# Output projection of the gated convolution: two pairs of tiles direct, six in Strassen's form

## The reference, cut to what matters

```python
def conv_mixer(h, w_in, conv_w, w_out):
    u, b_gate, c_gate, z = jnp.split(h @ w_in, 4, axis=-1)
    y = b_gate * causal_depthwise_conv(c_gate * u, conv_w)
    return (y * jax.nn.silu(z)) @ w_out
...
        x = x + rms_norm(y, norm_post[layer])
        h = rms_norm(x, xattn_norm_pre[layer])
        m = rms_norm(mem, mem_norm[layer])
        y = memory_cross_attention(h, m, m_w_q[layer], m_w_kv[layer], m_w_o[layer])
```

## Time and profile before

| What | us |
| --- | --- |
| Median of three runs | 2331.9 |
| Profiled execution | 2331.37 |
| Its span, first to last instruction | 2329.6 |
| Input projection in Strassen's form | about 1426 to 1977 |
| Output projection, direct | 1977.7 to 2153 |
| Norm, then opening of the cross attention's projection | 2153 to 2159.4 |

### The profile page before, as it was taken

How to read it: one execution, slowest core, us unless ns; L and a number is a source line. 1 busy time by engine, 2 the same in 40 slices (tenths; PEclk the granted TensorE clock), 3 DMA queues, 4 the chain that set the end, 5 groups by cost and what they waited for, 6 DMA issues and landing times.

```text
span 2329.6 us, 31140 instructions
## 1 busy us (share of the span) xinstructions
PE 2292.6 (98%) x12121; PEld 1919.0 (82%) x12121; DVE 1572.5 (68%) x2133; ACT 952.5 (41%) x1573; POOL 276.3 (12%) x213
## 2 busy tenths in 40 slices
PE   8999999999999999999999899999999999999998
PEld 6888888888787778888877788888888888888776
DVE  6676767674455658733385699888988898533855
ACT  5233333323344437522244364444444445322444
POOL 4000000001010101001040330000000100010400
PEclk9999999999999999999999899999999999999999
DMA  5322222223322324442222246767676666423222
GB/s 205 100 78 82 77 81 77 81 79 99 109 91 73 91 67 160 158 168 94 96 71 66 82 154 172 200 191 199 189 199 190 190 189 204 159 91 117 68 68 91
DMA packets 96958, 288.42 MB, mean 124 GB/s; under 512 B 18336, under 2 KB 21568, under 8 KB 96832
## 3 DMA queue, kind: packets, MB, share of 16 engines
q1 hardware_dynamic: 88288, 255.74, 33.0%
q0 software_dynamic: 8064, 29.36, 7.2%
q10 hardware_dynamic: 480, 1.59, 0.2%
HBM read 275.63 MB, written 11.03 MB: 123 GB/s over the span
## 4 chain that ended last, share of the span: by engine, by line
PE 95%; DVE 3%; ACT 1%; issue 1%; DMA 0%; POOL 0%; DVEq 0%; SPq 0%; ACTq 0%
PE acc L1154 17%; PE acc L1156 17%; PE acc L1155 17%; PE m L1649 10%; PE acc L1649 5%; PE m L1654 5%; PE acc L1654 3%; PE acc L1512 2%; PE acc L1513 2%; PE acc L1517 2%; DVE weights_lo L1681 1%; PE m L1328 1%; PE m L1336 1%; PE acc L1382 1%; PE acc L1384 1%
## 5 line engine op out<-in xcount | busy, mean ns | idle before, releaser
L1154 PE MATMUL acc<-input_hi_lo,weights_hi 128*128 128x512 f32 (+1 forms) x1880 | 743.0, 395 | 11.2 <-DVE weights_lo L1681 10.5
L1156 PE MATMUL acc<-input_hi_lo,weights_lo 128*128 128x512 f32 (+1 forms) x1880 | 720.3, 383 | 0.0
L1155 PE MATMUL acc<-input_hi_lo,weights_hi 128*128 128x512 f32 (+1 forms) x1880 | 719.5, 383 | 0.0
L1681 DVE TENSOR_TENSOR weights_lo<-weights_raw,weights_hi 128x1024 fp32r<-128x1024 f32 x288 | 399.4, 1398 | 178.7 <-ACT weights_hi L610 177.9
L1154 PEld LDWEIGHTS acc<-input_hi_lo,weights_hi 128*128 128x128 f32 x1880 | 354.1, 188 | 90.0 <-issue 14.8
L1156 PEld LDWEIGHTS acc<-input_hi_lo,weights_lo 128*128 128x128 f32 x1880 | 353.7, 188 | 71.2
L1155 PEld LDWEIGHTS acc<-input_hi_lo,weights_hi 128*128 128x128 f32 x1880 | 354.5, 189 | 64.6 <-issue 1.9
L610 ACT ACTIVATE weights_hi<-weights_raw 128x1024 fp32r<-128x1024 f32 x288 | 299.1, 1058 | 189.6 <-PE acc L1156 156.6
L1649 PE MATMUL m<-input_hi_lo,weights_hi 128*128 128x512 f32 x672 | 169.3, 394 | 1.2 <-issue 0.9
L1649 PEld LDWEIGHTS m<-input_hi_lo,weights_hi 128*128 128x128 f32 x672 | 120.7, 189 | 24.3 <-issue 2.6
L990 ACT ACTIVATE weights_hi<-weights_raw 128x1024 fp32r<-128x1024 f32 x85 | 89.9, 1059 | 88.6 <-PE m L1654 43.9
(11 more groups left out here) (376 smaller groups left out, 3455.4 us busy)
## 6 DMA issues: line engine op xcount, KB each, us to landing
weights_raw<-in_ab_w_in SPq DMA_DIRECT2D x126, 512.0 KB, 3.5
weights_raw<-in_c_w_in SPq DMA_DIRECT2D x73, 512.0 KB, 4.6
work<-in_c_w_in SPq DMA_DIRECT2D x42, 512.0 KB, 3.7
weights_raw<-in_m_w_kv SPq DMA_DIRECT2D x32, 512.0 KB, 3.6
weights_raw<-in_ab_w_out SPq DMA_DIRECT2D x32, 512.0 KB, 4.4
weights_raw<-in_m_w_q SPq DMA_DIRECT2D x32, 512.0 KB, 3.5
weights_raw<-in_c_w_out SPq DMA_DIRECT2D x32, 512.0 KB, 4.3
weights_raw<-in_c_w_in POOLq DMA_DIRECT2D x29, 512.0 KB, 7.5
```

Of the source, the lines that this page charges most:

```text
L1154: pe.matmul(out, w_hi[:, o:o + P], hi(kt), start=kt == first_kt, stop=False)
L1155: pe.matmul(out, w_hi[:, o:o + P], lo(kt), start=False, stop=False)
L1156: last = pe.matmul(out, w_lo[:, o:o + P], hi(kt), start=False, stop=kt == last_kt)
L1681: TTO(w_lo[:, s * CW:(s + 1) * CW], raw[:, c * CW:(c + 1) * CW], w_hi[:, s * CW:(s + 1) * CW].bitcast(F32), ALU.subtract).then_inc(lo_read ...
```

## The change

- The output projection runs pairs 0 and 1 directly and pairs 2 to 7 in Strassen's form. These are numbered q = 28 to 33, after the 28 of the input projection, and use the same functions, buffers, banks and semaphores. The host lays `c_w_out` out so that the halves of a pair are contiguous.
- While the two direct pairs run, VectorE and ScalarE make the sums of the input y (`turned_sums_out`, `turned_low_out`, `turned_high_out`, and `fourth_low_out` in the first Strassen pair), in X and in parts of Y and the work buffer.
- GpSimd issues the DMA sums of these pairs between its additions of squares: those of pair q after the squares of pair q - 2 have been added. ScalarE makes the squares of a pair during products 2 and 3 of the next one.
- The residual is reloaded in two halves: tiles 0 to 7 after product 2 of the last pair, 8 to 15 after its product 4. VectorE waits for the first half ahead of the first sum with the residual and GpSimd for the second ahead of tile 8.
- The first chunks of the next projection (C_Q1 on) are loaded and split during the last pair; the third is split after its last product. `last_chunk` isn't used here any more.

```diff
-C_Q1, P_Q1 = C_OUT1 + 32, P_OUT1 + 8
+C_Q1, P_Q1 = C_OUT1 + 8, P_OUT1 + 2
...
-S_PAIRS = 28
+S_PAIRS, OUT_PAIRS = 28, 6
...
+            def after_pairs(end, c):
+
+                q = end - 2 + c % 2
+                sp.wait_ge(s_lo, 7 * q + (5 if c < 2 else 3))
+                sp.wait_ge(s_sum["S4" if c < 2 else "S2"], q + 1)
...
-                if n == 0:
-                    sp.wait_ge(s_used, 7 * (S_PAIRS - 1) + 5)
+            for q in range(S_PAIRS, S_PAIRS + OUT_PAIRS):
+                s_loads(q)
+            for c in (0, 2, 1, 3):
+                j, kt0 = opening_chunk(c)
+                after_pairs(S_PAIRS + OUT_PAIRS, c)
+                load(dram["m_w_q"], 16 + 4 * j + kt0 // 4, C_Q1 + c)
+                if c == 2:
                     sp.wait_ge(x_kept, 16 * KT)
-                    for k in range(KT):
+                    sp.wait_ge(s_used, S_ALL - 7 + 3)
+                    for k in range(8):
                         sp.dma_start(xt(k), dram["x_kept"][k]).then_inc(x_back, 16)
-            sp.wait_ge(s_lo, S_CHUNKS)
+            sp.wait_ge(s_used, S_ALL - 7 + 5)
+            for k in range(8, KT):
+                sp.dma_start(xt(k), dram["x_kept"][k]).then_inc(x_back2, 16)
+            sp.wait_ge(s_lo, S_ALL)
...
+            def wino_out():
+
+                OA.round(2)
+                split(C_OUT1 + 4)
+                for n in (2, 0, 1):
+                    turned_high_out(0, n)
+                split(C_OUT1 + 5)
+                split(C_OUT1 + 6)
+                for n in (2, 0, 1):
+                    turned_high_out(1, n)
+                act.wait_ge(turn_in, 16)
+                for k in (0, 1):
+                    out_squares(k, (acc_free, 2 * P_OUT1 + k + 1))
+                split(C_OUT1 + 7)
+                for i in range(S_CHUNKS, S_CHUNKS + S_SLOTS):
+                    s_split(i)
+                for i in range(S_CHUNKS, S_ALL):
+                    q, pos = divmod(i, 7)
+                    n = q - S_PAIRS + 2
+                    product_copy(i, [(turn_lo, 16)] + ([OG("a11", 2)] if n == 7 else []))
+                    if i > S_CHUNKS and i + 2 < S_ALL:
+                        s_split(i + 2)
+                    if n == 2 and pos in (1, 2):
+                        turned_high_out(pos - 1, 3)
+                    if pos in (2, 3):
+                        k = 2 * n - 4 + pos
+                        if n == 7 and pos == 2:
+                            act.wait_ge(s_used, S_ALL - 7 + 2)
+                        out_squares(k, (acc_free, 2 * (P_OUT1 + 2)) if n == 2 else (s_ev, evacs(q - 1, "C21")))
+                    if i >= S_ALL - 2:
+                        act.wait_ge(s_used, i)
+                        split(C_Q1 + i - S_ALL + 2)
+                q = S_PAIRS + OUT_PAIRS - 1
+                out_squares(14, (s_ev, evacs(q, "C12")))
+                out_squares(15, (s_ev, evacs(q, "C21")))
+                act.wait_ge(s_used, S_ALL)
+                split(C_Q1 + 2)
...
-            out_phase(2, C_OUT1, P_OUT1, 4, lambda kt: YV(f"lo{kt}"))
+            NM.round(2)
+            for n in range(2):
+                for c in range(4):
+                    chunk(C_OUT1 + 4 * n + c, P_OUT1 + n, OUT1_TILES[c], KT - 1,
+                          ready=(lambda kt: YV(f"lo{kt}")) if n == 0 else None, first_kt=OUT1_TILES[0])
+            for q in range(S_PAIRS, S_PAIRS + OUT_PAIRS):
+                for pos in range(7):
+                    wino_product(q, pos)
+            pe.wait_ge(*OG("a13", 2))
+            ss_part(acc_sq, True, False).then_inc(*NM.did("last0"))
...
+            def wino_out():
+                turned_sums_out(0)
+                split(C_OUT1 + 5)
+                take_out(0)
+                turned_sums_out(1)
+                split(C_OUT1 + 6)
+                turned_low_out(0)
+                split(C_OUT1 + 7)
+                turned_low_out(1)
+                for i in range(S_CHUNKS, S_CHUNKS + S_SLOTS):
+                    s_split(i)
+                take_out(1)
+                for i in range(S_CHUNKS, S_ALL):
+                    if i > S_CHUNKS:
+                        evacuate_product((i - 1) // 7, (i - 1) % 7)
+                        if i + 2 < S_ALL:
+                            s_split(i + 2)
+                    q, pos = divmod(i, 7)
+                    if pos in (0, 2):
+                        weight_sum(q, ("S2", "S4")[pos // 2])
+                    if q == S_PAIRS and pos in (1, 2):
+                        fourth_low_out(pos - 1)
+                    if i >= S_ALL - 2:
+                        split(C_Q1 + i - S_ALL + 2)
+                evacuate_product(S_PAIRS + OUT_PAIRS - 1, 6)
+                split(C_Q1 + 2)
...
                 for k in range(KT - 2):
+                    if r == 2 and k >= 2 and k % 2 == 0 and k // 2 <= OUT_PAIRS:
+                        wino_sums(S_PAIRS + k // 2 - 1)
                     pool.wait_ge(*OA(f"s{k}", r))
```

More of the change, by code:

```diff
@@ L504, in cross_loads @@
             def cross_loads(l):
-                for c in range(16):
+                for c in range(4 * l, 16):
                     j, kt0 = opening_chunk(c)
@@ L535, in s_loads @@
                 s_load(q, 2, s_raw["r2"][q % 2], s_in["r2", q % 2])
[L536 to L539 removed]
+                if new == 0:
+                    sp.wait_ge(lo_ready, base + 13)
+                elif new == 1:
+                    sp.wait_ge(s_lo, 7 * first + 2)
                 else:
@@ L1653, in wino_product @@
                     o = s * CW + kt * P
-                    last = pe.matmul(high_half(out), w_lo[:, o:o + P], moving(pos, kt)[1], start=False, stop=kt == 7,
+                    last = pe.matmul(high_half(out), w_lo[:, o:o + P], moving(q, pos, kt)[1], start=False, stop=kt == 7,
                                      skip_group_check=True)
@@ L2560, in _, with turned_sums_out @@
             split(C_OUT1 + 3)
+            split(C_OUT1 + 4)
             last_input(12, 16)
-            out_phase(2, C_OUT1, P_OUT1, 4)
+            def turned_sums_out(b):
+                (low0, low1), (high0, high1) = ([four(Y, 4 * b + k, h) for h in range(2)] for k in (0, 8))
+                dve.wait_ge(s_used, S_CHUNKS)
+                for k in range(4 * b, 4 * b + 4):
+                    dve.wait_ge(y_back[k], 16)
+                TTO(four(third_out, 4 * b, 1), high1, low1, ALU.subtract).then_inc(turn_in, 1)
+                TTO(before_first(b), low0, low1, ALU.subtract).then_inc(turn_in, 1)
+                dve.wait_ge(turn_in, 8 + 4 * b + 2)
+                TTO(before_second(b), high1, before_first(b), ALU.add).then_inc(turn_in, 1)
+                dve.wait_ge(turn_in, 8 + 4 * b + 3)
+                TTO(fourths_out(b), before_second(b), high0, ALU.subtract).then_inc(turn_in, 1)
@@ new lines, in turned_low_out @@
+            def turned_low_out(b):
+                for n in (2, 0, 1):
+                    of = four(third_out, 4 * b, 1) if n == 2 else (before_first, before_second)[n](b)
+                    home_, k = (turned_o if n == 2 else turned_x), 4 * b + (0, 8, 0)[n]
+                    dve.wait_ge(turn_hi, 8 + 3 * b + (2, 0, 1).index(n) + 1)
+                    if n == 1:
+                        dve.wait_ge(turn_in, 8 + 4 * b + 4)
+                    STT(out=four(home_, k, 1), in0=of, scalar=-1.0 if n == 1 else 1.0,
+                        in1=four(home_, k, 0).bitcast(F32), op0=ALU.mult, op1=ALU.subtract).then_inc(turn_lo, 1)
@@ L2650, in _ @@
                     pool.wait_ge(*NV(f"y{k}", r))
+                    if r == 2 and k in (2, 8):
+                        pool.wait_ge(*((x_back, 16 * 8) if k == 2 else (x_back2, 16 * 8)))
                     pool.tensor_tensor(xt(k), xt(k), yt(k), ALU.add).then_inc(*NG.did(f"x{k}"))
```

180 lines of the change are left out of this document (113 added, 67 removed).

## The result

The changed kernel took **2340.4 us** (median of seven runs, 2338.6 to 2342.2), against 2331.9 for the kernel before, timed beside it: a ratio of 1.0035 (95% interval 1.0023 to 1.0047). It is 8.5 us slower, where the prediction had it 6.0 us faster and its range ended at 2336. The profiled execution has a span of 2338.5 us, 8.9 more than before.

A forecast was written before the change was run, and what follows sets the result against it. TensorE was taken to bound the kernel, PE instructions being 95% of the chain that ended last. Matmuls -13.2, tail +2.6 and DMA-sum waits +4.6 gave -6.0 us, a forecast of 2325.9 us, range 2320 to 2336.

The forecast's parts named there:

- Matmuls, -13.2: Output projection: six pairs go from 21.77 us direct to 19.57 us in Strassen's form, 13.2 us less.
- New sums and splits of the input, 0: Beside the two direct pairs: VectorE's and ScalarE's new work just fits; wait of 0 to 1 us, taken as 0.
- The ring: Strassen output pairs: each S1 DMA sum waits, through ScalarE, VectorE and GpSimd, for the one before; 4.6 us of waits.
- L: Time from issue to landing of S1's DMA sum beside SP's loads; taken as 9.9 us, range 9.7 to 10.4.
- 11.1 + L: Shortest pair length in the output stage: 11.1 us of other steps plus the sum's landing; binds above L = 8.5.
- the slack of the first ring: First later sum, issued 13.2 us into its pair: a landing up to 10.9 us is harmless once.
- Rival B: Software queue served behind the hardware queue's backlog: L = 12.5, waits 17.6 us, in all +9.6, 2341.5 us; chance 0.13.
- The forecast: Main case for the whole kernel: sums and loads share the DMA engines, -6.0 us, 2325.9 us; chance 0.40.
- Tail, +2.6: Last product to opening of the next projection: last evacuation, square and queued splits add 2.6 us (2.1 to 3.0).
- a late chunk C_Q1+1: Tail: its load, issued behind eight residual tiles, may land late and delay the last evacuation by up to 0.9 us.
- from the statistic to the opening 4.67 as now: Tail: from VectorE's statistic to the next projection's opening stays 4.67 us, unchanged.
- Residual, 0: End of the output projection: reloading the residual in two halves costs nothing, each asked for ahead of need.

The follow-up runs named there:

- experiment 1: Changed kernel with GpSimd issuing each output pair's DMA sums one pair earlier; 2322.3 us.
- (4): Changed kernel with GpSimd's additions of squares covering 16 of 512 columns, most of the norm's sum left out; 2323.4 us.
- experiment 9: Experiment 1 with splits reordered in the tail, chunk C_Q1+1 loaded before the residual, and VectorE's two splits waiting for GpSimd's power; 2320.4 us.
- 2: Changed kernel with a pair's DMA sums issued one addition earlier, between the even and odd square of the pair before; 2323.5 us.
- 6 to 10: On experiment 1: splits reordered, 2321.8; chunk before residual, 2322.9; both, 2321.4; then splits behind the power, 2320.4; then extra matmuls keeping TensorE busy, 2319.4 us.

## Why the prediction was wrong, step by step

- **Matmuls, -13.2.** Right: 19.57 us a pair in nine kernels, and 0.9 more for the long last chunk of before, which I had not counted.
- **New sums and splits of the input, 0.** Right in size: experiments 1 and 4 have no wait in the first pair with all of this work in place. The changed kernel's 2.4 us there come from full-length additions that fall on the S4 sum and its split (2.31 and 2.22 us): with small additions (4) the wait goes, and in experiment 1, where the S4 sum begins before the addition and takes 1.22, it goes too.
- **The ring.** The mechanism was right (its steps, and the lines that wait), the terms were not. This is the step that failed: the length of the ring was put in too short, and with it the waits, 4.6 us for 18.0. "12.4 + L" stood there as 11.1 + L: the S4 sum was put in at 1.22 and the addition at 1.29, each as it is when alone, though the ring itself places both beside work of the other engine. That is 1.6 us, less 0.3 for other steps. And L was taken as 9.9 by shares of bandwidth and measured 10.9 to 11.2. Together the excess of a late pair is 3.8 us in the mean (the periods of the sums are 23.25 to 23.43), not 1.4. By my own formula with the right constant, the waits begin at L = 7.2, not 8.5, and even the 7.5 of a sum without loads beside it would not have been quite free.
- **The price of the error.** Four late pairs at 3.8 are 15.2 us; the first pair's 2.4 and the second's 0.3 make it 18.0. The prediction had 4 x 1.4 and took off 1.0 for the slack of the first ring. That slack wasn't there: S1's sum for the first late pair is issued 15.5 us into the pair before (2060.57 against 2045.03), not 13.2, and that pair loses as much as the others. So of the 13.4 us that the waits were off, 9.6 are the longer ring, 2.7 the first two pairs and 1.0 the slack.
- **Rival B** names nearly the right time, 2341.5, but by luck. Its own terms, -13.2 + 2.6 + 17.6, are +7.0 and not +9.6, so 2338.9: the 2.6 of the tail was added twice. Its 17.6 us of waits come from a landing of 12.5 with 11.1 for the rest; the runs have 10.9 to 11.2 with 12.4. In the first 3 us of the backlog S1's sum got little, and then nearly half. The forecast and B each had half of it.
- **Tail, +2.6.** 3.6. The last evacuation ended 0.9 us later than drawn, the top of the bounds; 0.5 of that is in the 2.6. But the reason given, a late chunk C_Q1+1, is not that of the changed kernel: ScalarE had its high part ready at 2157.03, and VectorE, busy without a pause, came to its split only at 2158.20 and so to the last evacuation at 2159.33, 0.9 behind the last product. The chunk is late only where the last product comes sooner behind its load, as in experiment 1. The rest of the miss is "from the statistic to the opening 4.67 as now": it is 5.65 (2162.99 to 2168.64), since the rows of the norm take 2.07 us, not 1.16, with the granted clock at 0.55 from 2162 to 2168. TensorE had stood still for 2.3 us ahead of them, where before it was 1.4; in experiment 9 it is 1.4 again, and the rows take 1.20.
- **Residual, 0.** Right: no engine waits for it.
- **Chances.** The loss had 0.13, in one rival with a threshold at L = 11.1. The ring's rest of 11.1 had no bounds: with it even the measured L of 11.2 gives only 11.1 us of waits and 2332.4 us, and the range, which left out most of B, ended at 2336.

## What to carry to other kernels

When a DMA sum (or any long transfer) is issued behind work that itself needs the last one, write the ring down and compare its length with the period of the bottleneck; here issuing one addition earlier took 17 us off the kernel, and the whole change then gained 0.4 to 0.6% (experiments 1, 2 and 6 to 10). Durations in such a ring must be those beside the work that will lie next to them, not those of the engine alone. And a step of 1 us is to be read from the trace, at the place: the start of this stage alone moved by 2.5 us between executions of the same code.
